# A routed mixture of experts on one core: all paired experts first, whole-tile experts last

## The chip, the cores and the metric

The kernel runs on one core of a Trainium2 chip, in float32. The metric is the device time of one launch in microseconds (us). "Before" is the kernel as it stood, "after" is the kernel with the change.

## The reference, cut to what matters

The reference computes two layers of a hybrid block over 256 latent tokens and 256 context tokens of width 1024. Each layer has a mixing half (delta net, three kinds of attention) that the change does not touch, and a mixture of experts that it does:

```python
D_MODEL, N_EXPERTS, TOP_K, D_EXPERT, ROUTED_SCALE = 1024, 64, 6, 384, 2.5

def swiglu(x, w_gu, w_down):
    g, u = jnp.split(x @ w_gu, 2, axis=-1)
    return (jax.nn.silu(g) * u) @ w_down

# moe_ffn: scores = sigmoid(h @ router_w); the top 6 of scores + bias are chosen for each token;
# gates = chosen scores / their sum * 2.5
# routed = sum over the 6 chosen experts e of gate_e * swiglu(h, exp_w_gu[e], exp_w_down[e])
return routed + swiglu(h, shared_gu, shared_down)
```

Layer 0 runs it on all 512 tokens (4 tiles of 128), layer 1 on the 256 latent tokens only (2 tiles). Every layer reads the weights of all its 64 experts: w_gu is 1024 x 768 and w_down 384 x 1024, together 4.72 MB an expert and 302 MB a layer.

## The kernel before, in words

Five engines run their own instruction lists and wait on semaphores: TensorE (PE), VectorE (DVE), ScalarE (ACT), GpSimd (POOL) and SyncE (SP), which issues the weight loads.

**Units of work.** The mixture is a list of units `WORK[l]`. A shared unit is the shared expert on one tile of tokens. A routed unit is 128 gathered rows. The experts are sorted by how many tokens chose them: the first `WHOLE[l]` (16 in layer 0, 4 in layer 1) get a whole unit each, and the others are paired, two experts of at most 64 rows in one unit. Layer 0 so has 4 shared units, 24 pairs and 16 wholes, and layer 1 has 2 shared units, 30 pairs and 4 wholes. The order before is all shared units first, and then `work(l)`, which spreads the wholes evenly among the pairs. With P for a pair and w for a whole, layer 0 is `PPwPwPPwPwPPwPwPPwPwPPwPwPPwPwPPwPwPPwPw`, and layer 1 is `PPPPPPPPwPPPPPPPwPPPPPPPPwPPPPPPPw`.

**A unit on PE.** `unit_up(n)` multiplies the unit's transposed rows by w_gu, in two halves of the contraction ("lo", then "hi"; L1330). Then PE transposes the rows of the next unit (L1311), and `unit_down(n)` transposes the activation (L1341) and multiplies by w_down (L1350). A whole has 32 up matmuls and 12 down matmuls with 128 columns of the array in use. A pair has twice as many, each with 64 columns, one expert on each half of the array. ACT does the silu (L1564) and half of the result's copy. DVE does the product (L1941), the copy of the transposed rows (L2069, L2070) and the other half of the result's copy (L1947 for a shared unit, L2081 for a routed one). POOL gathers the rows two units ahead (L2238) and scatters the results (L2244).

**Weights.** They lie in 8 slots of 1.57 MB (one `CHUNK`). An expert takes three: lo, hi and down. SP walks through the routed units in order (L814). Chunk i goes to slot i % 8, and before it is issued SP waits until PE has used what the slot held: a lo after the lo half of its unit (`lo_used`), a hi after the hi half (`gu_psum`), a down after the down matmuls (`down_psum`). SP waits in order, so a chunk that waits holds back all behind it. The three chunks of the shared expert come first, and their slots are free only after the last shared unit.

**Routing beside the shared units.** While the first shared units run, DVE sorts the experts and makes the lists of rows: PE multiplies one-hots into a list by expert (`lists_by_expert`, L1253), DVE copies it (L2013), PE makes the list by unit (L1258), and DVE turns that into the indices POOL gathers by (L2017 to L2020). DVE then computes the gates (L2027 to L2031) and addresses for overflowing rows (L2035 to L2049). Only after both does it copy the first unit's transposed rows.

Of the kernel before, what the change touches and what calls it, by code (L numbers as in the profile page):

```python
# [13 lines left out]
P = 128  # L14
D = 1024
KD = D // P
# [17 lines left out]
NE = 64  # L34
TOPK = 6
# [6 lines left out]
HALF = P // 2  # L42
WHOLE = (16, 4)
UNITS = tuple((NE + w) // 2 for w in WHOLE)
CHUNK = 3072
SLOTS = 8
# [87 lines left out]
def build(nc, x, c, ctx, c_ctx, w_mod, b_mod, norm1_g, norm2_g, w_in, gdn_conv_w, gdn_a_log, gdn_dt_bias,  # L134
          gdn_norm_g, mla_qn_g, mla_kvn_g, mla_w_uq, mla_w_ukv, mla_qk_g, swa_qk_g, swa_sink, gqa_qk_g,
          w_out, router_w, router_bias, exp_w_gu, exp_w_down, shared_w_gu, shared_w_down, consts, out):
    with ExitStack() as stack:
# [431 lines left out]
        NSH = NOUT  # L569
        WORK = [[(None, (i,)) for i in range(NSH[l])] + work(l) for l in LAYERS]  # L570
        NW = [len(w) for w in WORK]
        NR = [NW[l] - NSH[l] for l in LAYERS]
        PARTS = ("lo", "hi", "down")
        CHUNKS = [[(n, part, j) for n, (_, ranks) in enumerate(WORK[l]) if n == 0 or n >= NSH[l]
                   for part in PARTS for j in range(len(ranks))] for l in LAYERS]
        SLOT_OF = [{c: i % SLOTS for i, c in enumerate(CHUNKS[l])} for l in LAYERS]
# [5 lines left out]
        slotT_psum = sig("slotT_psum", NR)  # L582
        slotT = sig("slotT", NR)
# [79 lines left out]
        def _(sp):  # L663
# [57 lines left out]
            for l in LAYERS:  # L721
# [98 lines left out]
                for n, (_, ranks) in enumerate(WORK[l]):  # L820
                    if n < NSH[l]:
                        continue
                    experts = [sp.value_load(eid[0:1, r:r + 1], min_val=0, max_val=NE - 1) for r in ranks]
                    for part in PARTS:
                        for j in range(len(ranks)):
                            if loaded >= SLOTS:

                                m, was, _ = CHUNKS[l][loaded - SLOTS]
                                m = max(m, NSH[l] - 1)
                                sp.wait_ge(free_by[was].sem, free_by[was].at(l, m + 1))  # L830
                            if loaded == SLOTS - 1:

                                sp.wait_ge(primed.sem, 1)
                            load_chunk((n, part, j), experts)
                            loaded += 1
# [28 lines left out]
        def _(pe):  # L864
# [69 lines left out]
            for l in LAYERS:  # L934
# [362 lines left out]
                def weights(n, part):  # L1297

                    n = n if n >= NSH[l] else 0
                    qs = [SLOT_OF[l][n, part, j] for j in range(len(WORK[l][n][1]))]  # L1300
                    for j, q in enumerate(qs):
                        pe.wait_ge(chunk_loaded[q].sem, chunk_loaded[q].at(l, SEQ_OF[l][n, part, j] + 1))
                    return qs

                def unit_transposed(n):
                    r = n - NSH[l]
                    pe.wait_ge(gathered[r % 2].sem, gathered[r % 2].at(l, r // 2 + 1))
                    if r:
                        pe.wait_ge(slotT.sem, slotT.at(l, r))
                    for k in range(KD):  # L1310
                        last = pe.transpose(ps[k // 4][:, tok(k % 4)], slots[r % 2].rearrange("p (d k) -> p k d", k=KD)[:, k, :], ident)  # L1311
                    last.then_inc(slotT_psum.sem, 1)

                def unit_up(n, between=None):
                    if n >= NSH[l]:
                        pe.wait_ge(slotT.sem, slotT.at(l, n - NSH[l] + 1))
                        src = hgT[(n - NSH[l]) % 2]
# [41 lines left out]
                unit_up(1)  # L1359
                lists_by_expert()  # L1360
                unit_down(1)
                lists_by_unit()
                for n in range(2, NSH[l]):
                    unit_up(n)
                    unit_down(n)
                unit_transposed(NSH[l])
                for n in range(NSH[l], NW[l]):
                    unit_up(n)
                    if n + 1 < NW[l]:
                        unit_transposed(n + 1)  # L1370
                    unit_down(n)
# [13 lines left out]
        def _(act):  # L1385
# [16 lines left out]
            for l in LAYERS:  # L1402
# [157 lines left out]
                for n in range(NW[l]):  # L1560
# [9 lines left out]
                    r = n - NSH[l]  # L1570
                    if n == 0:
                        act.wait_ge(h_stored.sem, h_stored.at(l, NOUT[l]))
                    if r >= 2:
                        act.wait_ge(scattered[r % 2].sem, scattered[r % 2].at(l, r // 2))
                    y = outs[r % 2] if r >= 0 else acc[:, OUT_TILES[l][n], :]
# [8 lines left out]
        def _(dve):  # L1584
# [56 lines left out]
            for l in LAYERS:  # L1641
# [301 lines left out]
                def shared_out(n):  # L1943
# [3 lines left out]
                    dve.tensor_copy(acc[:, OUT_TILES[l][n], 512:1024], ps[5][:]).then_inc(unit_y.sem, 1)  # L1947
# [73 lines left out]
                for n in range(2, NSH[l]):  # L2021
                    unit_times(n)
                    if n + 1 < NSH[l]:
                        shared_out(n)
# [8 lines left out]
                if NSH[l] > 2:  # L2033
                    shared_out(NSH[l] - 1)
                link(ts(base, rank, float(U_), float(HALF * U_ - U_ + W_), ALU.is_ge, ALU.mult))  # L2035
                link(tt(base, base, rank, ALU.add))
                link(tt(cnt, cnt, cap, ALU.subtract))
                link(red(cntmax[:, 0:1], cnt, AX, ALU.max))
                link(ts(cntmax[:, 1:2], cntmax[:, 0:1], float(P), None, ALU.add))
                link(dve.tensor_copy(maxcnt[0:1, 0:1], cntmax[0:1, 1:2]))  # L2040
                link(stt(adr[:, nt_, :], pos[:, nt_, :], float(U_), bc(base, 1, n_t), ALU.mult, ALU.add))
                link(stt(adr2[:, nt_, :], pos[:, nt_, :], float(NE), bc(K("experts"), 1, n_t), ALU.mult, ALU.add))
                link(stt(adr2[:, nt_, :], adr2[:, nt_, :], float(LIST1), adr[:, nt_, :], ALU.add, ALU.subtract))
                link(tt(adr2[:, nt_, :], adr2[:, nt_, :], over[:, nt_, :], ALU.mult))
                link(tt(adr[:, nt_, :], adr[:, nt_, :], adr2[:, nt_, :], ALU.add))
                for i in range(n_t):
                    link(tt(ohp, onehot[:, i], bc(adr[:, i, :], 1, TOPK), ALU.mult))
                    link(red(posk[:, i, 0:TOPK], ohp, AX, ALU.add))
                dve.tensor_copy(addr[:, nt_, 0:TOPK], posk[:, nt_, 0:TOPK]).then_inc(addr_ready.sem, 1)  # L2049
# [16 lines left out]
                def unit_copied(n):  # L2066
                    r = n - NSH[l]
                    dve.wait_ge(slotT_psum.sem, slotT_psum.at(l, r + 1))
                    dve.tensor_copy(hgT[r % 2][:, 0:4, :], ps[0][:].rearrange("p (k n) -> p k n", k=4))  # L2069
                    dve.tensor_copy(hgT[r % 2][:, 4:8, :], ps[1][:].rearrange("p (k n) -> p k n", k=4)).then_inc(slotT.sem, 1)  # L2070

                unit_copied(NSH[l])
                for n in range(NSH[l], NW[l]):
                    unit_times(n)
                    if n + 1 < NW[l]:
                        unit_copied(n + 1)
                    dve.wait_ge(down_psum.sem, down_psum.at(l, n + 1))
                    r = n - NSH[l]
# [31 lines left out]
        def _(pool):  # L2110
# [21 lines left out]
            for l in LAYERS:  # L2132
# [103 lines left out]
                def unit_in(r):  # L2236
                    u = WORK[l][NSH[l] + r][0]
# [4 lines left out]
                def unit_out(r):  # L2242
                    u = WORK[l][NSH[l] + r][0]
# [27 lines left out]
                pool.wait_ge(gu_psum.sem, gu_psum.at(l, NSH[l]))  # L2271
# [3 lines left out]
                for r in range(NR[l]):  # L2275
                    if r + 2 < NR[l]:

                        pool.wait_ge(slotT_psum.sem, slotT_psum.at(l, r + 1))
                        waited()
                        unit_in(r + 2)  # L2280
                    pool.wait_ge(unit_y.sem, unit_y.at(l, 2 * (NSH[l] + r) + 2))
# [38 lines left out]
```

## Time and profile before

| | |
|---|---|
| median of 3 runs | 3029.93 us (3028.95 to 3030.80) |
| the profiled execution | 3032.81 us |
| its span, first to last instruction | 3030.9 us |
| mean granted clock of PE | 0.904 |
| PE busy | 2432.6 us (80%) |
| DMA over the span | 776.00 MB, 256 GB/s |
| mixture of layer 0, routed units on PE | 775.88 to 1580.30 us |
| mixture of layer 1, routed units on PE | 2220.48 to 2978.72 us |

The profile was taken in one execution, and its times are from the start of the span. The busy time of PE is for pipelined matmuls, and the wait for a load shows on the matmul that needed it. The last two lines of the table are read from the first up matmul and the end of the last down matmul of each layer.

### The profile page before, as it was taken

Reading aid. Unit: us, or ns where it says so; the run is one execution under the profiler, and the core shown is the slowest. Engines: PE = TensorE matmul, PEld = TensorE weight load, DVE = VectorE, ACT = ScalarE, POOL = GpSimd, SP = SyncE. Lnnn points to the kernel's source line nnn. Section 1 sums busy time; section 2 is a strip of 40 time slices with the busy share of each in tenths; the row PEclk is TensorE's granted clock in tenths of the full one; section 3 lists DMA queues with packets and bytes.
Section 4 is the critical chain, followed back from the end, with each engine's and each line's share of the span. In section 5 each row is a group of like instructions: output and inputs, shape, how many; then the busy total and the mean of one; then the engine's idle time right before and its main releaser. Section 6 shows DMA issues by size and latency. Waiting matters only on the chain. (4 is left out here: it accounts for less than half of the span.)

```text
span 3030.9 us, 36674 instructions
## 1 busy us (share of the span) xinstructions
PE 2432.6 (80%) x15133; PEld 1334.9 (44%) x15133; DVE 800.4 (26%) x1601; ACT 425.1 (14%) x854; POOL 316.4 (10%) x374
## 2 busy tenths in 40 slices
PE   5978869999899888988870797929877888888882
PEld 2447625555444444444430356816543434444331
DVE  2214564324211111111015413574421111111112
ACT  1022323310000000000000203215100000000000
POOL 0015200000011111110100004300001111101000
PEclk8989978799999999999995898959989999999996
DMA  7010266333899999999956110001489999999992
GB/s 266 24 51 3 71 224 224 128 123 124 327 426 424 416 400 402 390 402 406 398 213 256 47 46 2 3 9 67 183 347 428 421 419 421 413 413 416 410 393 108
DMA packets 122428, 776.00 MB, mean 256 GB/s; under 512 B 34648, under 2 KB 45032, under 8 KB 65808
## 3 DMA queue, kind: packets, MB, share of 16 engines
q1 hardware_dynamic: 99216, 735.75, 60.1%
q0 software_dynamic: 23040, 37.82, 3.3%
q8 instruction: 125, 2.05, 0.3%
q14 instruction: 47, 0.39, 0.0%
HBM read 770.98 MB, written 44.44 MB: 269 GB/s over the span
## 5 line engine op out<-in xcount | busy, mean ns | idle before, releaser
L1330 PE MATMUL banks<-arena,htreg 128*64 128x384 f32 (+1 forms) x4288 | 905.5, 515 | 129.3 <-DMA arena<-in_exp_w_gu 119.5
L1330 PEld LDWEIGHTS banks<-arena,htreg 128*64 128x64 f32 (+1 forms) x4288 | 448.0, 155 | 594.9 <-issue 366.8
L1350 PE MATMUL banks<-arena,modreg 128*64 128x512 f32 (+1 forms) x1608 | 439.9, 607 | 74.2 <-DMA arena<-in_exp_w_down 32.5
L1941 DVE TENSOR_TENSOR modreg<-modreg,banks 128x384 f32<-128x384 f32 x80 | 44.3, 554 | 967.2 <-ACT modreg L1564 967.2
L1350 PEld LDWEIGHTS banks<-arena,modreg 128*64 128x64 f32 (+1 forms) x1608 | 165.4, 150 | 294.9 <-issue 294.9
L2244 POOL DMA_INDIRECT y_d<-modreg,lst x74 | 73.6, 994 | 1362.8 <-DVE modreg L2081 1346.5
L953 PE MATMUL banks<-arena,htreg 128*128 128x428 f32 x512 | 184.2, 522 | 0.0
L1564 ACT ACTIVATE modreg<-banks 128x384 f32<-128x384 f32 x80 | 39.2, 490 | 998.0 <-PE banks L1330 998.0
L2081 DVE COPY modreg<-banks 128x512 f32<-128x512 f32 x74 | 51.2, 692 | 437.0 <-PE banks L1350 437.0
L953 PEld LDWEIGHTS banks<-arena,htreg 128*128 128x128 f32 x512 | 97.3, 190 | 86.9 <-issue 86.9
L1576 ACT ACTIVATE modreg<-banks 128x512 f32<-128x512 f32 x74 | 44.2, 597 | 440.0 <-PE banks L1350 440.0
L907 PE MATMUL banks<-const,hreg 128*128 128x128 f32 x64 | 13.2, 387 | 107.1 <-DVE hreg L1633 107.1
L2238 POOL DMA_INDIRECT htreg<-h_d,lsg x74 | 76.7, 1036 | 199.5 <-DVE lsg L2020 89.0
L1311 PEld LDWEIGHTS banks<-const,htreg 128*128 128x128 f32 x592 | 73.6, 193 | 50.0 <-issue 32.3
L943 PE MATMUL banks<-htreg,arena 128*128 128x512 f32 x192 | 84.7, 603 | 13.5 <-SPq L622 12.8
L1311 PE MATMUL banks<-const,htreg 128*128 128x128 f32 x592 | 84.5, 286 | 12.0 <-DMA htreg<-h_d,lsg 12.0
L873 PE MATMUL banks<-modreg,crep 128*32 128x512 f32 x320 | 59.3, 829 | 39.1 <-DMA modreg<-in_w_mod 37.7
L1202 PE MATMUL banks<-arena,htreg 128*128 128x512 f32 x192 | 83.1, 592 | 0.0
L1158 PE MATMUL banks<-arena 64*128 64x512 f32 (+3 forms) x144 | 78.1, 627 | 2.3 <-ACTq L622 2.3
L2098 DVE SCALAR_TENSOR_TENSOR hreg<-arena,gate,hreg 128x1024 f32<-128x1024 f32 x36 | 46.3, 1285 | 69.8 <-DMA arena<-y_d 68.6
L943 PEld LDWEIGHTS banks<-htreg,arena 128*128 128x128 f32 x192 | 37.0, 194 | 60.1 <-issue 46.1
L1341 PE MATMUL banks<-const,modreg 128*128 128x128 f32 x240 | 49.1, 313 | 16.2 <-DVE modreg L1941 11.6
(377 smaller groups left out, 2298.0 us busy)
## 6 DMA issues: line engine op xcount, KB each, us to landing
arena<-in_exp_w_gu SPq DMA_DIRECT2D x256, 1536.0 KB
arena<-in_exp_w_down SPq DMA_DIRECT2D x128, 1536.0 KB
modreg<-in_w_mod SPq DMA_DIRECT2D x40, 1024.0 KB, 5.0
arena<-y_d SPq DMA_DIRECT2D x6, 3072.0 KB, 17.6
arena<-in_w_in SPq DMA_DIRECT2D x8, 1712.0 KB, 10.8
modreg<-mod_d SPq DMA_DIRECT2D x20, 512.0 KB, 6.3
arena<-in_w_out SPq DMA_DIRECT2D x2, 4096.0 KB, 13.6
arena<-in_w_mod SPq DMA_DIRECT2D x6, 1024.0 KB, 9.3
```

The lines of the kernel that those rows point to most:

```text
L873: last = mm(bank[32 * c_:32 * c_ + 32, :], crep[:, k, :], w[:, 512 * c_:512 * c_ + 512], start=(k == 0), stop=(k == KD - 1))
L943: last = mm(ps[ct % 2][:], win_qkv[:, k, tok(ct)], hT[:, k, :], start=(k == 0), stop=(k == KD - 1))
L953: last = mm(ps[2 + n % 4][:, 0:CW], hT[:, k, tok(t)], win[ch % 2][:, k, :], start=(k == 0), stop=(k == KD - 1))
L1158: mm(ps[s % 2][:, 0:nk * P], q_, k_, start=True, stop=True).then_inc(scores_psum.sem, 1)
L1202: last = mm(ps[2 + n % 2][:], mixT[:, k, tok(t)], wout[:, k, 512 * half:512 * half + 512], start=(k == 0), stop=(k == KD - 1))
L1311: last = pe.transpose(ps[k // 4][:, tok(k % 4)], slots[r % 2].rearrange("p (d k) -> p k d", k=KD)[:, k, :], ident)
L1330: last = mm(ps[2 + half][rows, 0:DE], src[:, k, rows], up4[q][:, i, DE * half:DE * (half + 1)], start=(k == 0), stop=(k == KD - 1))
L1341: last = pe.transpose(ps[6][:, tok(k)], act_.rearrange("p (f k) -> p k f", k=KE)[:, k, :], ident)
L1350: last = mm(ps[4 + half][rows, :], actT[:, k, rows], dn3[q][:, k, 512 * half:512 * half + 512], start=(k == 0), stop=(k == KE - 1))
L2081: dve.tensor_copy(outs[r % 2][:, 512:1024], ps[5][:]).then_inc(unit_y.sem, 1)
L2238: pool.indirect_dma_start(out=slots[r % 2], out_offset=None, in_=h_d, in_offset=bass.IndirectOffsetOnAxis(ap=lsg1[:, u:u + 1], axis=0), bo ...
L2244: pool.indirect_dma_start(out=y_d, out_offset=bass.IndirectOffsetOnAxis(ap=lst1[:, u:u + 1], axis=0), in_=outs[r % 2], in_offset=None, bou ...
```

## The change

Three things change in the mixture.

1. The order. In layer 0 the units are shared 0, shared 1, whole, shared 2, whole, shared 3, then all 24 pairs, then the other 14 wholes. In layer 1 they are the 2 shared units, all 30 pairs, then the 4 wholes. A shared unit that comes after the first routed one (numbers 2 and 3 of layer 0) takes its input through the same transpose and copy as a routed unit, from h in place of gathered rows.
2. The slots. A chunk goes to the slot whose present chunk is used up first in the order of work, in place of slot i % 8. In layer 1 this is the same assignment. In layer 0 the shared expert's three slots stay taken until shared unit 3, now the sixth unit.
3. The lists. `lists_by_unit` moves ahead of `unit_down(1)` on PE and its four DVE operations ahead of `unit_times(1)`. In layer 1 `lists_by_expert` moves in between the two halves of `unit_up(1)`. POOL's first gather needs the second shared unit's up and no longer the last one's. The overflow addresses move behind the copy of the first transposed rows.

```diff
+        EARLY = 2
         def work(l):
             whole = [(u, (u,)) for u in range(WHOLE[l])]
             paired = [(u, (u, u + UNITS[l] - WHOLE[l])) for u in range(WHOLE[l], UNITS[l])]
-            order = []
-            for i in range(len(paired)):
-                order.append(paired[i])
-                while whole and (len(order) - i) * len(paired) <= (i + 1) * WHOLE[l]:
-                    order.append(whole.pop(0))
-            return order + whole
+            order = [whole.pop(0) for _ in range(NOUT[l] - EARLY)]
+            return order + paired + whole
+
+        def with_shared(l):
+            routed = work(l)
+            order = [(None, (i,)) for i in range(EARLY)]
+            for i in range(EARLY, NOUT[l]):
+                order += [routed.pop(0), (None, (i,))]
+            return order + routed
...
-        SLOT_OF = [{c: i % SLOTS for i, c in enumerate(CHUNKS[l])} for l in LAYERS]
+        freed = lambda l, c: (c[0] or LAST_SHARED[l], PARTS.index(c[1]))
+
+        def ring(l):
+            slot_of, held = {}, {}
+            for i, c in enumerate(CHUNKS[l]):
+                q = i if i < SLOTS else min(held, key=lambda q: freed(l, held[q]))
+                slot_of[c], held[q] = q, c
+            return slot_of
+
+        SLOT_OF = [ring(l) for l in LAYERS]
...
-                                m, was, _ = CHUNKS[l][loaded - SLOTS]
-                                m = max(m, NSH[l] - 1)
-                                sp.wait_ge(free_by[was].sem, free_by[was].at(l, m + 1))
+                                q = SLOT_OF[l][n, part, j]
+                                was = in_slot(l, q)[SEQ_OF[l][n, part, j] - 1]
+                                by = free_by[was[1]]
+                                sp.wait_ge(by.sem, by.at(l, freed(l, was)[0] + 1))
...
                 unit_down(0)
                 ranks()
-                unit_up(1)
-                lists_by_expert()
+                unit_up(1, between=lists_by_expert if n_t == 2 else None)
+                if n_t > 2:
+                    lists_by_expert()
+                lists_by_unit()
                 unit_down(1)
-                lists_by_unit()
-                for n in range(2, NSH[l]):
-                    unit_up(n)
-                    unit_down(n)
-                unit_transposed(NSH[l])
-                for n in range(NSH[l], NW[l]):
+                unit_transposed(EARLY)
+                for n in range(EARLY, NW[l]):
                     unit_up(n)
                     if n + 1 < NW[l]:
                         unit_transposed(n + 1)
                     unit_down(n)
...
-                unit_times(1)
                 dve.wait_ge(slot_hot_used.sem, slot_hot_used.at(l, TOPK * n_t))
                 dve.tensor_copy(listT, ps[1][lo64, 0:P]).then_inc(listT_ready.sem, 1)
-                shared_out(1)
...
                 ts(lsg1[:, 0:U_], lst1[:, 0:U_], 3, None, ALU.logical_shift_right).then_inc(lists_ready.sem, 1)
+                unit_times(1)
+                shared_out(1)
...
-                unit_copied(NSH[l])
-                for n in range(NSH[l], NW[l]):
+                unit_copied(EARLY)
+                overflow_addresses()
+                for n in range(EARLY, NW[l]):
                     unit_times(n)
                     if n + 1 < NW[l]:
                         unit_copied(n + 1)
+                    if is_shared(l, n):
+                        shared_out(n)
+                        continue
...
                 pool.wait_ge(lists_ready.sem, lists_ready.at(l, 1))
-                pool.wait_ge(gu_psum.sem, gu_psum.at(l, NSH[l]))
+                pool.wait_ge(gu_psum.sem, gu_psum.at(l, EARLY))
```

## Rows read from the trace of the kernel before

**Rows 1.** The page: busy tenths and GB/s in 40 equal slices
```profile
PE   5978869999899888988870797929877888888882
DMA  7010266333899999999956110001489999999992
GB/s 266 24 51 3 71 224 224 128 123 124 327 426 424 416 400 402 390 402 406 398 213 256 47 46 2 3 9 67 183 347 428 421 419 421 413 413 416 410 393 108
```
**Rows 2.** Busy time by stretch (PE, PEld, DVE, ACT, POOL), PE clock, DMA share, GB/s
```profile
905.95:1518.05 612.10, 543.15 (x2443) 268.14 (x2443) 74.95 (x120) 47.33 (x90) 80.43 (x80) 0.97 0.99 404
2214.00:2230.00 16.00, 11.49 (x52) 5.50 (x54) 3.12 (x6) 0.00 (x0) 0.99 (x1) 0.64 0.26 77
2299.13:2395.87 96.74, 76.15 (x397) 36.25 (x397) 10.13 (x16) 6.32 (x12) 12.02 (x12) 0.95 1.01 426
2299.13:2955.03 655.90, 546.45 (x2739) 263.27 (x2740) 73.22 (x116) 45.76 (x87) 68.45 (x68) 0.95 1.00 414
```
**Rows 3.** Timeline of PE: a whole and a pair, neither waiting long
```profile
911.25 10.59 PE L1330 MATMUL banks<-arena,htreg 128*128 128x384 f32 x32
924.26 5.39 PE L1350 MATMUL banks<-arena,modreg 128*128 128x512 f32 x12 [0.63 <-issue]
929.58 10.54 PE L1330 MATMUL banks<-arena,htreg 128*64 128x384 f32 x64
942.77 5.37 PE L1350 MATMUL banks<-arena,modreg 128*64 128x512 f32 x24 [0.86 <-DMA arena<-in_exp_w_down]
```
**Rows 4.** Timeline of PE: down matmuls at the ends of both stretches
```profile
905.95 5.37 PE L1350 MATMUL banks<-arena,modreg 128*64 128x512 f32 x24 [2.53 <-DMA arena<-in_exp_w_down]
1518.05 5.37 PE L1350 MATMUL banks<-arena,modreg 128*64 128x512 f32 x24 [0.78 <-ACT modreg L1568]
2299.13 5.37 PE L1350 MATMUL banks<-arena,modreg 128*64 128x512 f32 x24 [0.78 <-ACT modreg L1568]
2955.03 5.37 PE L1350 MATMUL banks<-arena,modreg 128*64 128x512 f32 x24 [0.78 <-ACT modreg L1568]
```
**Rows 5.** Timeline of PE: the last unit's down in each layer
```profile
1573.21 7.09 PE L1350 MATMUL banks<-arena,modreg 128*128 128x512 f32 x12 [0.63 <-issue]
2973.33 5.39 PE L1350 MATMUL banks<-arena,modreg 128*128 128x512 f32 x12 [0.63 <-issue]
```
**Rows 6.** Timelines of PE, DVE and POOL where layer 0's routed units start
```profile
721.51 5.39 PE L1350 MATMUL banks<-arena,modreg 128*128 128x512 f32 x12 [0.63 <-issue]
775.88 13.41 PE L1330 MATMUL banks<-arena,htreg 128*64 128x384 f32 x64 [8.26 <-DVE htreg L2070]
727.54 0.19 DVE L2017 TENSOR_SCALAR stat<-banks 128x40 f32<-128x40 f32 x1
728.22 0.18 DVE L2020 TENSOR_SCALAR lsg<-lst 128x40 uint32<-128x40 uint32 x1
758.60 0.55 DVE L2027 TENSOR_TENSOR modreg<-modreg,arena 128x384 f32<-128x384 f32 x1
763.74 0.18 DVE L2031 SCALAR_TENSOR_TENSOR gate<-gate,arena 128x24 f32<-128x24 f32 x1
774.54 0.68 DVE L2069 COPY htreg<-banks 128x512 f32<-128x512 f32 x1
758.36 1.03 POOL L2238 DMA_INDIRECT htreg<-h_d,lsg  x1 [72.17 <-PE banks L1330]
```
**Rows 7.** The same where layer 1's routed units start
```profile
2196.17 3.10 PE L1253 MATMUL banks<-arena,modreg 128*64 128x128 f32 x24
2217.12 1.97 PE L1311 MATMUL banks<-const,htreg 128*128 128x128 f32 x8 [10.86 <-DMA htreg<-h_d,lsg]
2220.48 13.03 PE L1330 MATMUL banks<-arena,htreg 128*64 128x384 f32 x64 [1.38 <-DVE htreg L2070]
2208.25 1.08 POOL L2238 DMA_INDIRECT htreg<-h_d,lsg  x1 [88.98 <-DVE lsg L2020]
```
**Rows 8.** All gathers: us from issue to landing
```profile
DMA to landing us min/median/max: 4.2/12.7/14.4
```

More of the change, by code:

```diff
@@ L561, in work @@
             paired = [(u, (u, u + UNITS[l] - WHOLE[l])) for u in range(WHOLE[l], UNITS[l])]
-            order = []
-            for i in range(len(paired)):
-                order.append(paired[i])
-                while whole and (len(order) - i) * len(paired) <= (i + 1) * WHOLE[l]:
-                    order.append(whole.pop(0))
-            return order + whole
-        NSH = NOUT
-        WORK = [[(None, (i,)) for i in range(NSH[l])] + work(l) for l in LAYERS]
-        NW = [len(w) for w in WORK]
-        NR = [NW[l] - NSH[l] for l in LAYERS]
+            order = [whole.pop(0) for _ in range(NOUT[l] - EARLY)]
[6 more added lines that the diff above has]
+            return order + routed
+        WORK = [with_shared(l) for l in LAYERS]
+        NW = [len(w) for w in WORK]
+        is_shared = lambda l, n: WORK[l][n][0] is None
+        ROUTED_AT = [[n for n in range(NW[l]) if not is_shared(l, n)] for l in LAYERS]
+        LAST_SHARED = [max(n for n in range(NW[l]) if is_shared(l, n)) for l in LAYERS]
+        NR = [len(r) for r in ROUTED_AT]
+        NQ = [n - EARLY for n in NW]
         PARTS = ("lo", "hi", "down")
-        CHUNKS = [[(n, part, j) for n, (_, ranks) in enumerate(WORK[l]) if n == 0 or n >= NSH[l]
+        CHUNKS = [[(n, part, j) for n, (_, ranks) in enumerate(WORK[l]) if n == 0 or not is_shared(l, n)
                    for part in PARTS for j in range(len(ranks))] for l in LAYERS]
-        SLOT_OF = [{c: i % SLOTS for i, c in enumerate(CHUNKS[l])} for l in LAYERS]
+        freed = lambda l, c: (c[0] or LAST_SHARED[l], PARTS.index(c[1]))
[6 more added lines that the diff above has]
+        SLOT_OF = [ring(l) for l in LAYERS]
         in_slot = lambda l, q: [c for c in CHUNKS[l] if SLOT_OF[l][c] == q]
@@ L581, in build @@
         lo_used = sig("lo_used", NW)
-        slotT_psum = sig("slotT_psum", NR)
-        slotT = sig("slotT", NR)
+        slotT_psum = sig("slotT_psum", NQ)
+        slotT = sig("slotT", NQ)
         gu_psum = sig("gu_psum", NW)
@@ L1305, in unit_transposed @@
                 def unit_transposed(n):
[L1306 to L1309, printed above, removed]
+                    q = n - EARLY
+                    if is_shared(l, n):
+                        src = h[:, OUT_TILES[l][WORK[l][n][1][0]], :].rearrange("p (k d) -> p k d", k=KD)
+                    else:
+                        r = ROUTED_AT[l].index(n)
+                        pe.wait_ge(gathered[r % 2].sem, gathered[r % 2].at(l, r // 2 + 1))
+                        src = slots[r % 2].rearrange("p (d k) -> p k d", k=KD)
+                    if q:
+                        pe.wait_ge(slotT.sem, slotT.at(l, q))
                     for k in range(KD):
-                        last = pe.transpose(ps[k // 4][:, tok(k % 4)], slots[r % 2].rearrange("p (d k) -> p k d", k=KD)[:, k, :], ident)
+                        last = pe.transpose(ps[k // 4][:, tok(k % 4)], src[:, k, :], ident)
                     last.then_inc(slotT_psum.sem, 1)
                 def unit_up(n, between=None):
-                    if n >= NSH[l]:
-                        pe.wait_ge(slotT.sem, slotT.at(l, n - NSH[l] + 1))
-                        src = hgT[(n - NSH[l]) % 2]
+                    if n >= EARLY:
+                        pe.wait_ge(slotT.sem, slotT.at(l, n - EARLY + 1))
+                        src = hgT[(n - EARLY) % 2]
                     else:
@@ L1569, in _ @@
                     act.wait_ge(down_psum.sem, down_psum.at(l, n + 1))
-                    r = n - NSH[l]
                     if n == 0:
                         act.wait_ge(h_stored.sem, h_stored.at(l, NOUT[l]))
-                    if r >= 2:
-                        act.wait_ge(scattered[r % 2].sem, scattered[r % 2].at(l, r // 2))
-                    y = outs[r % 2] if r >= 0 else acc[:, OUT_TILES[l][n], :]
+                    if is_shared(l, n):
+                        y = acc[:, OUT_TILES[l][WORK[l][n][1][0]], :]
+                    else:
+                        r = ROUTED_AT[l].index(n)
+                        if r >= 2:
+                            act.wait_ge(scattered[r % 2].sem, scattered[r % 2].at(l, r // 2))
+                        y = outs[r % 2]
                     fn(y[:, 0:512], ps[4][:], ACT.Copy).then_inc(unit_y.sem, 1)
@@ L2032, in _ @@
                          ALU.mult, ALU.mult))
[L2033 to L2049, printed above, removed]
+                def overflow_addresses():
+                    link(ts(base, rank, float(U_), float(HALF * U_ - U_ + W_), ALU.is_ge, ALU.mult))
+                    link(tt(base, base, rank, ALU.add))
+                    link(tt(cnt, cnt, cap, ALU.subtract))
+                    link(red(cntmax[:, 0:1], cnt, AX, ALU.max))
+                    link(ts(cntmax[:, 1:2], cntmax[:, 0:1], float(P), None, ALU.add))
+                    link(dve.tensor_copy(maxcnt[0:1, 0:1], cntmax[0:1, 1:2]))
+                    link(stt(adr[:, nt_, :], pos[:, nt_, :], float(U_), bc(base, 1, n_t), ALU.mult, ALU.add))
+                    link(stt(adr2[:, nt_, :], pos[:, nt_, :], float(NE), bc(K("experts"), 1, n_t), ALU.mult, ALU.add))
+                    link(stt(adr2[:, nt_, :], adr2[:, nt_, :], float(LIST1), adr[:, nt_, :], ALU.add, ALU.subtract))
+                    link(tt(adr2[:, nt_, :], adr2[:, nt_, :], over[:, nt_, :], ALU.mult))
+                    link(tt(adr[:, nt_, :], adr[:, nt_, :], adr2[:, nt_, :], ALU.add))
+                    for i in range(n_t):
+                        link(tt(ohp, onehot[:, i], bc(adr[:, i, :], 1, TOPK), ALU.mult))
+                        link(red(posk[:, i, 0:TOPK], ohp, AX, ALU.add))
+                    dve.tensor_copy(addr[:, nt_, 0:TOPK], posk[:, nt_, 0:TOPK]).then_inc(addr_ready.sem, 1)
```

28 lines of the change are left out of this document (12 added, 16 removed).

## The prediction, made before the changed kernel was run

> **What bounds the kernel now.** I read the page's slices first [rows 1]. In slices 11 to 20 and 30 to 39 the DMA engines are nine tenths busy or more and move about 400 to 428 GB/s. These are the two mixtures, and PE is nearly as busy there. Which of the two ends a unit last is a question of the kind of unit, so I took stretches next [rows 2] and then PE's timeline [rows 3, 4].
>
> PE needs the same time for either kind. From the up matmuls of a whole to those of the next pair it is 929.58 - 911.25 = 18.33 us, and from the whole's down to the pair's 942.77 - 924.26 = 18.51 us, which holds 0.86 us of waiting for weights [rows 3]. I take 18.3 us for a unit of either kind. A whole brings the weights of one expert through the DMA and a pair those of two.
>
> The DMA's price of an expert comes from long stretches between down matmuls [rows 4]. In layer 1, from 2299.13 to 2955.03, lie 26 pairs and 3 wholes, 55 experts: 655.90 / 55 = 11.93 us an expert, with the DMA at 1.00 [rows 2]. In layer 0, from 905.95 to 1518.05, lie 18 pairs and 12 wholes, 48 experts: 612.10 / 48 = 12.75 us, with the DMA at 0.99 and 404 GB/s. So a pair costs the DMA about 24 to 25.5 us, more than PE's 18.3, and a whole costs it 12 to 13 us, less than PE's 18.3. In layer 0 the even mix balances: 64 x 12.75 = 816 us of DMA beside 40 x 18.3 = 732 us of PE, and the DMA's surplus in a whole pays its deficit in the next pair. Layer 1 is bound by the DMA, and PE waits inside its pairs.
>
> **The change part by part: order.** Eight slots hold 2.7 experts, so the DMA can't run ahead of PE by more than about one pair. If all pairs come first, they run at the DMA's pace, with PE idle some 6 us in each. The wholes at the end run at PE's pace, with the DMA idle some 6 us in each. Neither idle time can be handed to the other. That is the main term.
>
> *Price of a pair in a run of pairs.* Layer 1 shows such a run: the four pairs up to 2395.87 take 96.74 / 4 = 24.19 us each at 426 GB/s, and its whole stretch gives 2 x 11.93 = 23.85 [rows 2]. Layer 0 carries twice the tokens, so twice the gathered and scattered rows, and its mean is 2 x 12.75 = 25.50. That mean includes wholes, which have the most rows, and the pairs alone have fewer. I take 24.6 us for layer 0, between 23.85 and 25.50, and 23.85 for layer 1.
>
> *Layer 0, where the routed units start* [rows 6]. Before, the list matmul stood behind down 1, and now it stands ahead of it. Its own chain (copy of the list, one matmul, DVE from 727.54 to 728.40) delays down 1 by some 2.5 us: it starts at 724.0 and ends at 729.4. POOL can gather from about 722.5 and no longer at 758.36. In layer 1 the transposes that waited for the first gather started 2217.12 - 2208.25 = 8.9 us after its issue and took 2.0 us [rows 7], so here the rows are in and transposed by about 733.4. DVE however has its half of the result's copy, the gates and then the first unit's two copies in line behind down 1: 0.7 us, 763.92 - 758.60 = 5.3 us, and twice 0.7. That is later, so DVE decides. The overflow addresses, which lie between 763.92 and 774.54 with a copy among them, now follow under an up of 10.6 us. So the first routed up starts near 736.9, not at 775.88. With the half clock after such a gap an up took 13.41 us in place of 10.54 [rows 3, 6], which I add: 2.9 us.
>
> But only two shared units are done by then. Whole, shared, whole and shared take 4 x 18.3 + 2.9 = 76.1 us, so the first pair starts at 813.0. A pair was started at 775.88 before, 37 us earlier, and what came in exchange are the two wholes, 36.6 us. So the 38.6 us between the two first routed ups are nothing but the two shared units moved, plus about 1 us.
>
> *DMA in that stretch.* Five slots turn over there, since three hold the shared weights until 813. Those five are full by 727 as before, and then chunks go out one at a time as whole 1 and whole 2 give them back: 3 for whole 2's last and pair 1's first two, then 5 more, the last being pair 2's first lo near 811. From about 815 the DMA is busy without a gap, and it owes the rest of pairs 2 to 24: 5 chunks and 22 pairs, (22 + 5/6) x 24.6 = 561.7 us. The last pair's weights are in at 1377, its down ends 5.4 us later at 1382, and 14 wholes at 18.3 us add 256.2: the layer's units end at 1638.6. Before they ended at 1573.21 + 7.09 = 1580.3 [rows 5]. **Layer 0: +58 us.**
>
> *Layer 1, end.* The last pair's down stood at 2955.03. Three wholes stood ahead of it, and their 3 x 11.93 = 35.8 us of DMA now come later: 2919.2. Down and four wholes follow, 5.4 + 4 x 18.3 = 78.6, so 2997.8 against 2973.33 + 5.39 = 2978.7: +19.1 us.
>
> *Layer 1, start* [rows 7]. `lists_by_expert` (3.1 us) goes between the halves of up 1, and the list by unit is made some 7 us sooner. The gather goes out near 2201 in place of 2208.25 and lands, at the 8.9 us before, near 2210. Down 1 ends some 2.5 us later at 2208.3. DVE then has its copy and the gates of two tiles in place of four (some 3.5 us) ahead of the copies of the transposed rows, so the up starts near 2213.5 in place of 2220.48. SP's next loads wait for the lo half of this up, and the DMA, which stood at 0.26 from 2214 to 2230 for lack of free slots [rows 2], starts again so much earlier: -7.5 us, clock included. The bounds are 0 (the gather takes the median of 12.7 us and more [rows 8]) and -10. **Layer 1: 19.1 - 7.5 = +11.6 us.**
>
> *Other edits.* Transposing shared units 2 and 3 through PE and DVE costs nothing: it takes the place that lies under the wait for the product in every routed unit. The slot rule is the old one wherever no shared slot is held. ACT's and POOL's orders follow the units, and their waits have 18 us of cover.
>
> **Sum.** 58 + 12 = +70 us. The profiled execution took 3032.81 and the median is 3029.93, so 3102.7 on the one and 3100 on the other. I give the median's scale.
>
> **The Trainium skill on the DMA.** The stretches of both layers ran at 404 to 426 GB/s [rows 2]. The Trainium skill, "DMA: Bandwidth & Descriptors", section Bandwidth, gives a measured 425 GB/s for large loads on one core and a fabric ceiling of 435. By 425, two experts' 9.44 MB take an estimated 22.2 us, below every pair seen here; that is the rival "cheap pairs" in its most favourable form, and the rows with four pairs in a row speak against it.
>
> **Rivals.**
> - *Cheap pairs (faster).* Without wholes between them, pairs stream at the best rate with row traffic hidden: 9.44 MB at 426 GB/s [rows 2] is 22.15 us. That takes 22.8 x 2.45 = 56 us off layer 0 and about 26 x 1.7 = 44 off layer 1, so 3000. For it: layer 0's mix has a lower rate, 404, than pairs in a row, 426. Against it: those pairs in a row took 24.19 us each at that very rate. It beats the old kernel once the 49 pairs cost 70 / 49 = 1.4 us less each than I take.
> - *Dear pairs.* Layer 0's price of 12.75 us an expert is the rate beside scatters and not the wholes' rows: 25.5 a pair, 22.8 x 0.9 = +21, so 3121.
> - *The start gives nothing in layer 1.* The gather lands late, +7.5: 3107.
> - *A start that loads more.* The first stretch of layer 0 leaves the DMA less idle than I count. All the gap from 727 to 815 less 8 chunks of 4.1 us is 55 us; half of it is 3073.
> - *Slow clock.* PE's granted clock averages 0.95 in the layer 1 stretch [rows 2], and with longer waits it may stay at 1.2 GHz through a pair, whose up and down then take 10.5 + 5.4 us more, 34.2 in place of 18.3. That is 10 us over the DMA's price, for 49 pairs 490 us, and for a tenth of them 49, so 3149. The Trainium skill, "TensorE: Matmul & The Clock Gate", section "HAM oscillation", describes loops that wait on loads and fall to the low clock at every tile. The pairs of layer 1 wait the same way and kept 0.95, so I give it little.
>
> **How the numbers follow.** Forecast as summed 0.66, dear pairs 0.15, late gather 0.08, more loaded at the start 0.05, slow clock 0.02, cheap pairs 0.04. The forecast's own range is 3083 to 3117 (layer 0's pair between 24.0 and 25.2, layer 1's end within 5). To hold 8 in 10 with the dear pairs and half of the fuller start, I give 3072 to 3124. A change of 0.2% is 6 us, about what a measurement of this kernel tells from none. Only cheap pairs can bring that about: faster 0.04, same 0.01, slower 0.95.
>
> **What would show it.** In the changed profile: in layer 0 the pairs' downs stand 24 to 25 us apart with PE waiting for in_exp_w_gu and the DMA at 1.0. Behind them stand 14 wholes 18.3 us apart, with the DMA near 0.7 and the clock at 1.00. The first routed up is near 737 and the first pair near 813. In layer 1 the last four downs are 18.3 us apart and the first up is near 2213.5 plus layer 0's delay. Wrong would be: pairs under 23 us apart, wholes that wait, or a first pair long before 800.

## The result, and the profile after

The changed kernel takes 3106.74 us (median of 4 runs, 3103.42 to 3108.76) against 3029.44 for the one before (median of 4, 3025.36 to 3030.80). The ratio is 1.0254, with a 95% interval of 1.0238 to 1.0269. It is 77 us slower; the forecast was 70, with 3100 in a range of 3072 to 3124.

The page of the changed kernel, slices as in [rows 1], and its waits of PE for gate and up weights:

```profile
PE   5979859998977787779992497947897888888893
DMA  6100175415799999998854310001389999999972
GB/s 259 38 35 3 69 269 198 165 50 191 305 428 427 424 408 399 402 398 331 298 206 189 113 46 1 3 9 58 119 367 428 423 421 424 417 418 412 421 323 101
```
```profile
PE banks L1355 <- DMA arena<-in_exp_w_gu: 187.5, 95, 3.8
```

In layer 0 the slices now split into two kinds. In slices 12 to 18 the DMA is at 9 and PE mostly at 7, and in slices 19 to 21 PE is at 9 and the DMA falls from 8 to 5. In slices 11 to 20 of [rows 1] both were at 8 or 9. PE waits 187.5 us for these weights over the whole program, and 119.5 before (the line of `unit_up` in the page of before). The same split in stretches of the changed kernel, columns as in [rows 2]:

```profile
742.00:815.00 73.00, 69.32 (x219) 38.68 (x219) 14.37 (x27) 5.79 (x12) 4.05 (x4) 0.98 0.56 195
865.43:1387.04 521.61, 401.36 (x2080) 189.84 (x2080) 53.20 (x84) 33.18 (x63) 63.23 (x63) 0.94 1.00 412
1406.96:1642.55 235.59, 222.79 (x708) 125.62 (x708) 30.58 (x50) 20.53 (x39) 24.26 (x24) 1.00 0.71 260
2360.00:2973.16 613.16, 502.10 (x2574) 239.22 (x2575) 65.86 (x104) 41.08 (x78) 63.43 (x63) 0.94 1.01 420
2991.47:3045.82 54.35, 50.71 (x157) 28.17 (x158) 6.14 (x10) 4.74 (x9) 3.99 (x4) 1.00 0.38 148
```

The first row is the stretch with the two wholes and the shared units 2 and 3. The second row is 21 pairs of layer 0 and the fourth is 26 of layer 1, each counted from one pair's down matmuls to a later pair's: 24.84 and 23.58 us a pair, with the DMA full. The third row is 13 steps from whole to whole, 18.12 us each, with the DMA at 0.71, and the fifth is three such steps at the end of layer 1, with the DMA at 0.38. PE's timeline in the changed kernel at the places of [rows 4 to 7]: start of layer 0's routed units, first pair, last pair, first and last whole, then the same ends in layer 1.

```profile
724.73 7.08 PE L1375 MATMUL banks<-arena,modreg 128*128 128x512 f32 x12 [0.63 <-issue]
739.15 13.57 PE L1355 MATMUL banks<-arena,htreg 128*128 128x384 f32 x32 [6.46 <-DVE htreg L2090]
814.83 10.54 PE L1355 MATMUL banks<-arena,htreg 128*64 128x384 f32 x64
1387.04 6.99 PE L1375 MATMUL banks<-arena,modreg 128*64 128x512 f32 x24 [1.52 <-DMA arena<-in_exp_w_down]
1406.96 5.39 PE L1375 MATMUL banks<-arena,modreg 128*128 128x512 f32 x12 [0.63 <-issue]
1642.55 7.08 PE L1375 MATMUL banks<-arena,modreg 128*128 128x512 f32 x12 [0.63 <-issue]
...
2246.70 7.08 PE L1375 MATMUL banks<-arena,modreg 128*128 128x512 f32 x12 [0.67 <-ACT modreg L1591]
2270.87 7.08 PE L1375 MATMUL banks<-arena,modreg 128*128 128x512 f32 x12 [0.63 <-issue]
2279.38 1.16 PE L1336 MATMUL banks<-const,htreg 128*128 128x128 f32 x8 [1.42 <-DMA htreg<-h_d,lsg]
2282.91 13.07 PE L1355 MATMUL banks<-arena,htreg 128*64 128x384 f32 x64 [2.37 <-DVE htreg L2090]
...
2973.16 5.37 PE L1375 MATMUL banks<-arena,modreg 128*64 128x512 f32 x24 [1.35 <-DMA arena<-in_exp_w_down]
3045.82 7.07 PE L1375 MATMUL banks<-arena,modreg 128*128 128x512 f32 x12 [0.63 <-issue]
```

To compare the layers free of what drifts ahead of them, I count from the down matmuls of shared unit 0 to the end of the last unit. They start at 697.19 and 2179.97 before, and at 698.24 and 2246.70 after.

| | before | after | difference |
|---|---|---|---|
| layer 0, from shared unit 0's down to the end of units | 883.1 | 951.4 | +68.3 |
| layer 1, the same | 798.8 | 806.2 | +7.4 |
| all else in the span | 1349.0 | 1347.3 | -1.7 |
| span | 3030.9 | 3104.9 | +74.0 |

### The profile page after: what moved, and what is told of

Same layout as the page of the kernel before. It is cut to its first block and busy times, and to the rows that moved or that the text cites. A ratio compares the mean times of both kernels' runs of the same rounds, so it can differ in the third digit from the quotient of the medians.

```text
span 3104.9 us, 36711 instructions
## 1 busy us (share of the span) xinstructions
PE 2458.1 (79%) x15149; PEld 1356.8 (44%) x15149; DVE 801.6 (26%) x1605; ACT 425.3 (14%) x854; POOL 316.1 (10%) x374
## 5 line engine op out<-in xcount | busy, mean ns | idle before, releaser
L1355 PE MATMUL banks<-arena,htreg 128*64 128x384 f32 (+1 forms) x4288 | 925.6, 524 | 196.4 <-DMA arena<-in_exp_w_gu 187.5
L1355 PEld LDWEIGHTS banks<-arena,htreg 128*64 128x64 f32 (+1 forms) x4288 | 468.8, 157 | 660.9 <-issue 386.2
L1967 DVE TENSOR_TENSOR modreg<-modreg,banks 128x384 f32<-128x384 f32 x80 | 44.3, 554 | 1041.6 <-ACT modreg L1587 1041.6
```

## The experiments

"Theory" below is the one of the forecast: pairs run at the DMA's pace and wholes at PE's, and eight slots can't carry the idle time of the one to the other. Each kernel ran beside the kernel before on the same chip. Not all experiments ran on one chip; where two of them are compared by their medians, note that the kernel before took 3029.4 to 3032.9 us beside them. "Layer 0 took" and "layer 1 took" mean the measure of the table above, in the profiled execution.

**1. Spread the wholes again, all else as changed.**

```diff
-            return order + paired + whole
+            W, lead = len(whole), len(order)
+            for i in range(len(paired)):
+                order.append(paired[i])
+                while whole and (len(order) - lead - i) * len(paired) <= (i + 1) * W:
+                    order.append(whole.pop(0))
+            return order + whole
```

> The changed kernel with its wholes spread among the pairs again in both layers (the two wholes among the shared units of layer 0 stay); slots, lists and early start as changed. Theory 'two idle times' (run of pairs leaves PE idle, run of wholes leaves DMA idle, and 8 slots can't carry one into the other): the loss goes, and the start of layer 1 keeps its gain of some 4 us, so 3020 to 3032, about 3025. Rival 'the start' (the interleaved shared units and the new slot rule cost the time, by keeping three slots and starting pairs 37 us later): still 3080 or more.

Measured 3032.62 us (10 runs), ratio 1.0005 (0.9994 to 1.0015). The whole loss is gone, so the order makes it. The time is 8 us over the expected 3025 and just outside its range of 3020 to 3032: the expected gain over the kernel before is missing. Layer 1 took 789.3 us, 9.4 less than before, but layer 0 took 892.3, 9.2 more. With spread order the changed start wins in the one layer and loses in the other.

**2. The order alone, on the kernel before.** Its `work` returns `paired + whole`.

> The kernel before with one edit: the routed units are all pairs and then all wholes; shared units first, slots and lists as before. Theory 'two idle times': about the changed kernel's time, 3095 to 3112 (layer 0 +60: last pair near 1347, 16 wholes of 18.1 behind it; layer 1 +11). Rival 'the start': near 3030.

Measured 3112.43, ratio 1.0272 (1.0248 to 1.0297). The one edit gives the loss and slightly more, since the gain of layer 1's start is missing. "The start" is out as its cause. The time is just over the expected 3095 to 3112. In its trace layer 0's last pair came at 1352.71, 6 us behind the expected 1347. Layer 0 took 951.2 us, 68.1 more than before (60 expected), and layer 1 took 809.7, 10.9 more (11 expected).

**3. Spread in layer 1 only.**

> The changed kernel with the spread order back in layer 1 only; layer 0 keeps pairs first. Theory: layer 0 holds most of the loss (58 in the forecast, 69 by the end of its units in the two traces), layer 1 the rest, so 3085 to 3102. If the loss were spread like the counts of pairs (24 and 30), 3065 or so.

Measured 3089.22, ratio 1.0187 (1.0167 to 1.0206). Against the changed kernel, the total is 3106.74 - 3089.22 = 17.5 us less, and against experiment 1 it is 3089.22 - 3032.62 = 56.6 more. The traces say where that lies. Layer 1 took 794.5 us here and 806.2 in the changed kernel, so its order is worth 11.7, as in experiment 2. Some 3 us more lie in layer 0, which took 948.2 in place of 951.4 with the same order: the down matmuls of the last pair and of the last whole ran at the full granted clock here and at a mean of 0.76 there. Layer 0's order is worth 948.2 - 892.3 = 55.9, close to the 56.6 of the medians.

**4. Wholes ahead of the pairs.** `return order + whole + paired` in both layers.

> The changed kernel with the remaining wholes ahead of the pairs in both layers. Theory 'two idle times': the order of the two runs does not matter, since what is lost is the overlap between them: within 10 us of the changed kernel, 3097 to 3117. Rival 'the tail' (the loss is that the last loads are in long before the last unit ends, so units that need much DMA should come last): most of the loss goes, under 3050.

Measured 3103.44, ratio 1.0232 (1.0210 to 1.0253), within 4 us of the changed kernel. So it is no matter of the tail. Layer 0's two runs in this kernel's trace, wholes and then pairs, in the columns of [rows 2]:

```profile
880.00:1060.00 180.00, 170.89 (x548) 96.81 (x547) 24.45 (x40) 15.77 (x30) 30.10 (x30) 1.00 0.82 293
1100.00:1640.00 540.00, 427.09 (x2180) 200.51 (x2179) 56.34 (x89) 34.98 (x67) 51.33 (x51) 0.93 0.98 406
```

In the first the DMA has room (0.82) and PE none, in the second it is the reverse, as in the changed kernel with the order turned round.

**5. Half a run.** Experiment 1 with the last 7 wholes of layer 0 at the end.

```diff
+            last = [whole.pop() for _ in range(7)][::-1] if l == 0 else []
...
-            return order + whole
+            return order + whole + last
```

> The kernel with spread order, but the last 7 wholes of layer 0 in a run at the end (14 in the changed kernel; layer 1 spread). Theory: each whole in the run costs what PE takes over the DMA's price, some 4 to 5.5 us, so about half of the 57 us that 14 of them cost in layer 0: 3056 to 3072. If only the long run of pairs with its wait counted, under 3045; if any run at all cost the whole, 3085.

Measured 3064.99, ratio 1.0113 (1.0093 to 1.0134). It is 32.4 us over experiment 1 for 7 wholes in a run, where 14 cost 56.6. That is 4.6 and 4.0 us for each whole in the run: the loss goes by their number. The size can be worked out, as an estimate. In experiment 1's spread order, 20 pairs and 12 wholes of layer 0 took 662.1 us (905.12 to 1567.26). With 24.84 us for each pair, 13.8 are left for a whole. A whole in a run takes 18.12, which is 4.3 more.

**6. Take the surplus of the pairs away.** In the changed kernel the second expert of a pair gets only the first quarter of its weights, and the rest is left out.

```diff
+                    if j == 1:
+                        dst, src = dst[:, 0:CHUNK // 4], src[:, 0:CHUNK // 4]
                     sp.dma_start(dst, src).then_inc(chunk_loaded[q].sem, 16)
```

> The changed kernel with only the first quarter of each chunk of a pair's second expert loaded (the rest of its weights is left out). A pair then costs the DMA 1.25 experts, some 15 us, under PE's 18.3. Theory: all pairs at 18.3, PE bound from end to end, 2800 to 2835. Rival: another wait than the loads sets the pairs' 24 us (the gathers or scatters): hardly below 3060.

Measured 2817.03, ratio 0.9297 (0.9278 to 0.9315). Its layer 0, pairs and then wholes:

```profile
846.00:1264.00 418.00, 398.73 (x2241) 203.97 (x2237) 57.48 (x91) 35.80 (x68) 69.17 (x69) 1.00 0.95 362
1285.00:1500.00 215.00, 203.53 (x648) 114.81 (x646) 28.14 (x46) 18.62 (x36) 22.22 (x22) 1.00 0.69 251
```

The pairs' downs now stand 18.26 us apart, with the granted clock at 1.00. The DMA is still at 0.95, an estimated 17.3 us of each pair's 18.26 where 15 had been expected, so it is only just under PE's pace. In layer 0 gathers and scatters are the same as ever, so they do not set the pairs' 24 us by themselves: it takes the loads. What rows add to the loads is the subject of experiment 9.

**7. The same cut with spread order.**

> The same cut of the loads in the kernel with spread order. Theory: with pairs and wholes both under PE's pace the order is worth nothing, so within 6 us of the changed kernel with the same cut, where it was worth 74 with full loads. Rival (the run of wholes is slow by itself): still 50 or more faster than that one.

Measured 2822.47, ratio 0.9308 (0.9285 to 0.9330). With both kinds of unit under PE's pace the spread order is 5 us slower than the runs, within the expected 6, where with full loads it was 74 faster. The run of wholes is not slow by itself. It is even a little better: from down to down it is 18.12 us from a whole to a whole and 18.26 from a pair to a pair, but 18.30 from a pair to a whole and 18.43 from a whole to a pair.

**8. What else could be in the price of a pair: the list scatters.** POOL writes 24 and 12 lists' entries in 4-byte packets beside the first routed units. Here they go beside the last.

```diff
-                    if 2 <= r < 2 + TOPK * n_t:
-                        listing(r - 2)
+                    late = NR[l] - TOPK * n_t - 2
+                    if late <= r < late + TOPK * n_t:
+                        listing(r - late)
```

> The changed kernel with POOL's 24 and 12 scatters of list entries (4-byte packets) moved from the first routed units to the last ones: in layer 0 the pairs 13 to 24 and the wholes carry them, and pairs 1 to 12 none. Tells what part of layer 0's 24.8 us a pair they are. Theory: small, 0.3 us a pair, so pairs 4 to 12 at 24.5 and total within 8 us of the changed kernel. Rival: they make layer 0's pairs dearer than layer 1's 23.6, so pairs without them at 23.8 and 10 to 15 us less in all.

Measured 3102.03, ratio 1.0234 (1.0217 to 1.0252). Layer 0's pairs 3 to 12, now free of them, took (1086.28 - 863.78) / 9 = 24.72 us, and 24.53 with them in the changed kernel. The expected 0.3 us a pair does not show, and the total is 5 us under the changed kernel's, within the expected 8. They are no part of the price that could be seen.

**9. The gathered and scattered rows.** The changed kernel with both bounds at 0, so that every row but row 0 is skipped, and y_d filled from other data at the start (the lines for that are left out here).

```diff
-            rows_bound = pool.to_reg(NT * P - 1)
-            codes_bound = pool.to_reg(NT * P * CODES - 1)
+            rows_bound = pool.to_reg(0)
+            codes_bound = pool.to_reg(0)
```

> The changed kernel with the indirect row transfers cut to nearly nothing: gathers and scatters skip every row but row 0 (the routed rows are left out; all else is computed as before), and y_d is filled once from other data at the start of the program, which delays layer 0's mixing and the total by some 50 to 90 us. To be read is the price of a pair, and not the total. Theory: layer 0's pairs (24.84 us, 24.53 for the early nine and 25.07 for the late twelve) are dearer than 9.44 MB at the best rate because of rows: without them 22.1 to 22.6 in both layers, early and late alike. Rival: the lower rate of the late pairs (402 GB/s against 425) comes from where the weights lie: then the late twelve stay 0.5 us or more above the early nine.

One execution, 3051.56 us, of which the total says little. Two stretches of layer 0's pairs and one of layer 1's, 10, 10 and 26 pairs:

```profile
933.04:1155.22 222.18, 185.94 (x990) 90.20 (x991) 25.35 (x40) 15.80 (x30) 30.11 (x30) 0.96 1.01 427
1155.22:1377.40 222.18, 185.94 (x991) 90.48 (x991) 25.35 (x40) 15.80 (x30) 30.10 (x30) 0.96 1.01 427
2342.42:2918.86 576.44, 480.16 (x2574) 233.47 (x2575) 65.88 (x104) 41.08 (x78) 63.57 (x63) 0.97 1.01 427
```

22.22, 22.22 and 22.17 us a pair, early and late alike. So rows cost 24.84 - 22.22 = 2.6 us a pair in layer 0 and 23.58 - 22.17 = 1.4 in layer 1, which has half the tokens.

In the changed kernel the early nine pairs of layer 0 (865.43 to 1086.20) took 24.53 us each with the DMA at 426 GB/s, and the late twelve (to 1387.04) took 25.07 at 402 GB/s. The late pairs' extra goes with the rows too, though they carry fewer of them: the software queue, which gathers and scatters, moved 0.71 MB for each early pair and 0.53 for each late one. Where the weights lie is out as its reason.

The bytes that the queues moved account for a part of the 2.6 us. In the 521.61 us of the 21 pairs they were 202.04 MB of the hardware queue, where 21 pairs need 198.2, and 12.73 MB of the software queue. At the 427 GB/s seen without rows, the rows' own bytes are an estimated 1.4 us a pair, and the weights moved beyond those of the 21 pairs 0.4. The rest is a lower rate, 412 for 427 GB/s. How rows lower it, most of all for the late pairs, I did not settle.

The rule cited in the forecast finds its number here: the Trainium skill, "DMA: Bandwidth & Descriptors", section Bandwidth, has 425 GB/s for large loads, an estimated 22.2 us for a pair's weights, and the trace without rows agrees, with 22.2 us at 427 GB/s. The pairs of the real kernel run at 24.84 and 23.58 us, so the rival built on that price stayed out.

**10. A version that beats both.** Experiment 1 is slower than the kernel before in layer 0, and I suspected the stretch beside the shared units. Two pairs go there in place of two wholes, the wholes are spread, and in layer 1 the last whole moves ahead of five pairs.

```diff
-            order = [whole.pop(0) for _ in range(NOUT[l] - EARLY)]
-            return order + paired + whole
+            order = [paired.pop(0) for _ in range(NOUT[l] - EARLY)]
+            W, lead = len(whole), len(order)
...
+            if l == 1:
+                order.insert(len(order) - 6, order.pop())
+            return order + whole
```

> The changed kernel with spread wholes again, with two pairs (not two wholes) among the shared units of layer 0, and with five pairs behind the last whole of layer 1. In the run with spread order layer 0 ended some 12 us later than before and layer 1 took 9 us less. Theory: beside the shared units a whole gives back 3 slots and a pair 6, so the DMA gets more done there; by a count of chunks layer 0 ends some 20 us earlier than with wholes there, and the tail of layer 1 gains up to 6: 3004 to 3018. Rival: what costs in that stretch is the late first pair and its slots, held by the shared weights until the sixth unit; then it stays near 3030.

Measured 3004.07, ratio 0.9911 (0.9891 to 0.9931): 27 us faster than before, 103 faster than the change, and at the lower end of the expected 3004 to 3018. Layer 0's first stretch in experiment 1 (first fence) and here (second):

```profile
736.00:824.00 88.00, 80.82 (x276) 44.14 (x278) 20.86 (x44) 6.31 (x12) 4.04 (x4) 0.95 0.55 192
```
```profile
734.00:822.00 88.00, 80.09 (x360) 39.12 (x362) 21.55 (x45) 6.31 (x12) 4.04 (x4) 0.96 0.74 298
```

PE is as busy in both, and the DMA moves 298 GB/s in place of 192. Layer 0 took 871.4 us, 21 less than in experiment 1 and 11.7 less than before. Layer 1 took 785.8, 13 less than before. Its tail's share in that is not sharp: it is 3.5 us against experiment 1 and 8.7 against experiment 3. Both have the old tail, but the granted clock in the shared units' down matmuls was high in the one and low in the other, as it was low here.

**11. The same with the list scatters late.**

> The version with two pairs among the shared units, spread wholes and pairs at the end of layer 1 (3004 before), with the list scatters moved to the last units of each layer. If they cost the bound DMA 0.3 us each where they stand, moving them changes nothing in a layer that is bound by the DMA throughout (3000 to 3008). If they only hurt beside the first units, up to 8 less.

Measured 3004.12, ratio 0.9904 (0.9888 to 0.9921): no difference. That alone does not tell a cost that the bound DMA pays wherever the scatters stand from no cost; experiment 8's pairs, which were no cheaper without scatters beside them, speak for no cost.

## Why the prediction was right

**The main term held.** Experiments 1 to 5 show that it is the order, that each of its two runs idles one resource, whichever comes first, and that its cost goes by the number of wholes in a run. Experiments 6 and 7 show the cause: once a pair's loads are under PE's pace, the spread order gains nothing. That it is the eight slots that keep the two idle times apart rests on the count (less than three experts fit) and was not tested: no run changed their number.

**Layer 0 was sized too small: +58 forecast, +68.3 measured.** The first routed up was forecast at 736.9 and came at 739.15, and the first pair at 813.0 and came at 814.83. This execution stood 1.05 us late at shared unit 0, so the start was about 1 us off: down 1 took 7.08 us for 5.39, at a granted clock of 0.76. The last pair's down, forecast at 1377, came at 1387.04. That is the mis-sized term: the time of the pairs. I took 24.6 between two means, and 21 pairs show 24.84, which is 5.0 us. The other 5 us were lost ahead of these 21: 1.05 is the lateness, and the DMA was not full from 815 on as I had counted. From 815 to 865.43 it was at 0.98 and 396 GB/s, and its hardware queue moved the weights of 1.95 pairs, 25.9 us for each. Thirteen steps from whole to whole were 18.12 us each, not 18.3, and gave 2.3 back. I had taken the 18.3 from a whole beside a pair, for want of a row with two wholes in a row. The low clock (0.76) in the last pair's and the last whole's down took 3.3.

**Layer 1 was sized too large: +11.6 forecast, +7.4 measured.** Both of its terms were. *The end's term was 19.1, and the order is worth 11 to 12 there:* 10.9 by experiment 2 against the kernel before, 11.7 by the changed kernel against experiment 3. I had taken 3 x 11.93 = 35.8 us for what three wholes ahead of the last pair cost. From shared unit 0's down to the last pair's down it is 775.1 us before and 726.5 after; less the 4.3 of the start, moving the wholes took 44.3 off. The 26 pairs show 23.58 us each against the 23.85 that I took from a stretch with three wholes in it, which is 7.0 of these 8.5. *The start's term was -7.5, and 4.3 were won:* the first routed up came 36.2 us after shared unit 0's down, and 40.5 before. Both shared downs took 7.08 us there, at a granted clock of 0.76, which I had not counted. In experiment 1 they took 5.39, and the first routed up came 33.5 us after shared unit 0's down, 7.1 sooner than before. The gate sums on DVE were the last to end ahead of the copies, as forecast, but only just: the first transposes had waited for the gather too (1.42 us).

**The errors cancel in part, and that is luck.** Layer 0 is 10 us over its term and layer 1 is 4 under, so the two together gave +75.7 where the sum had 70. The total came closer than layer 0 alone did. What is left between these 75.7 and the 77 lies in the rest of the span and between runs.

**Readings of the forecast that were not exact.** Slices 11 and 30 of [rows 1] are at 8, with 327 and 347 GB/s, and not nine tenths busy. The two first routed ups lie 39.0 us apart in the forecast and not 38.6. "Below every pair seen here" holds for means over several pairs: single steps of the kernel before took 22.1 us. Neither the sum nor a bound rests on these.

**The rivals.** "Cheap pairs" failed by its own row: 24.84 and 23.58 us in the mean, not 22.2, and experiment 9 shows that rows make the difference. "Dear pairs" (25.5) was wrong as a mean, but the late twelve of layer 0 with 25.07 came near it. "A start that loads more" did not happen: from 727 to 815 the hardware queue moved 13.03 MB, 8.3 chunks where I had counted 8. "Slow clock" did not happen: 0.94 in the pairs, and a wait inside each of them. "The start gives nothing in layer 1" was half true: 4.3 us of the 7.5.

**What I had not asked.** Two shared units among two wholes keep the shared weights' three slots some 50 us longer (to 809.51 + 5.39, the down of shared unit 3, where before all shared units were done ahead of 775.88), and each whole gives back only three chunks. With spread order that start is a loss of 9 us in layer 0 (experiment 1), and the same start with pairs is a gain of 12. With all pairs first it is neither: layer 0 took 951.4 us in the changed kernel and 951.2 with the old start (experiment 2). Two wholes fewer stand in the run behind the pairs there, which by experiment 5 is worth an estimated 8 to 9 us. The forecast counted the chunks of that stretch and did not ask which units should stand there.

## What to carry to other kernels

Where two kinds of work are bound by different resources and the buffer between the resources is small (here 8 slots, less than three experts), spread them. In a run, each item costs its own time less what it adds when spread (here 18.12 us less an estimated 13.8; 4.0 to 4.6 were measured), and it costs about that at either end of the stage. Price each kind for each resource from stretches that hold only that kind, and with the neighbours that it will have. Beside work that loads nothing, put the kind that gives back the most buffers (here 21 us in layer 0, experiment 10 against experiment 1).

## What the runs showed of the hardware

- Rows gathered and scattered by index beside large loads cost more than their bytes. In the stretches of pairs the software queue moved 0.61 MB a pair in layer 0 (12.73 MB for 21) and 0.34 in layer 1 (8.80 for 26), an estimated 1.4 and 0.8 us at 427 GB/s. They cost 2.6 and 1.4 us a pair. Moving the scatters of 4-byte entries (36 of them) away from the first pairs changed nothing that could be measured, in two kernels.
- Without the rows the loads ran at 427 GB/s for 576 us on end, 22.2 us for 9.44 MB.
- A unit of 128 columns behind another took 18.12 us and one of two times 64 columns behind another 18.26, and between the two kinds it was 18.30 to 18.43 (all at a granted clock of 1.00).
- PE that waited up to 3.8 us at a time in layer 0's pairs kept a mean granted clock of 0.94. Some halves of an up took 6.7 to 8.4 us there in place of 5.38.
